# Splitting the first attention's projections into three fp32r products each

## The reference

```
xn = rmsnorm(h, attn_norm[0])                   # 256 x 1024
proj = xn @ fox_w_in                            # 1024 x (3*1024 + 16)
q, k, v = 16 heads of 64 each; f_logit = last 16 columns + b_f
cum = cumsum(log_sigmoid(f_logit), axis=tokens)
s = q @ k.T / 8 + (cum[t] - cum[s]), causal softmax, o = p @ v
h = h + o @ fox_w_o                             # 1024 x 1024
h = h + (silu(hn @ w_gate) * (hn @ w_up)) @ w_down      # hn = rmsnorm(h, ffn_norm[0]), width 2816
```

## Time and profile before

| | |
|---|---|
| Median of 3 runs | 1963.29 us (1955.23 to 1964.63) |
| Profiled execution | 1963.11 us, span 1961.3 us |
| TensorE busy | 1734.0 us, 88% of the span |
| VectorE busy | 1019.6 us, 52% |
| ScalarE busy | 510.2 us, 26% |
| GpSimd busy | 279.1 us, 14% |
| Mean granted clock of TensorE | 0.949 of full |

### The profile page before, as it was taken

The page is one execution under the profiler, slowest core; times in us unless marked ns, Lnnn a source line. Parts: engine busy times, 40 slices in busy tenths (PEclk is TensorE's granted clock), DMA queues, the critical chain, the costliest instruction groups (busy, mean ns, idle before and its releaser), DMA issues.

```text
span 1961.3 us, 22190 instructions
## 1 busy us (share of the span) xinstructions
PE 1734.0 (88%) x7497; PEld 1181.4 (60%) x7497; DVE 1019.6 (52%) x2438; ACT 510.2 (26%) x1012; POOL 279.1 (14%) x264
## 2 busy tenths in 40 slices
PE   7998999889989999799999899968878889788876
PEld 4784999856648999587565468543434434344332
DVE  1234555533435554445734311377776667776765
ACT  1342444212324443143211001122222212222222
POOL 0000000000000000000000000045434343333540
PEclk8999999999998999899999999989989999898998
DMA  5253566501336565133322325099999999999996
GB/s 173 77 169 103 167 192 183 167 16 44 96 103 181 180 184 182 31 126 124 105 110 80 115 78 189 25 371 420 420 421 421 422 421 421 421 421 421 422 421 255
DMA packets 209713, 435.30 MB, mean 222 GB/s; under 512 B 11649, under 2 KB 145153, under 8 KB 175745
## 3 DMA queue, kind: packets, MB, share of 16 engines
q0 software_dynamic: 36864, 268.45, 33.0%
q1 hardware_dynamic: 171760, 166.06, 26.5%
q10 hardware_dynamic: 1040, 0.13, 0.0%
HBM read 433.53 MB, written 1.05 MB: 222 GB/s over the span
## 4 chain that ended last, share of the span: by engine, by line
PE 72%; DMA 16%; DVE 7%; issue 3%; ACT 1%; POOL 0%; DVEq 0%; SPq 0%; POOLq 0%; ACTq 0%
PE ps L484 40%; DMA OT<-in_peer_uv,IX 15%; PE ps L1220 11%; PE ps L645 6%; PE ps L925 3%; PE ps L938 2%; PE ps L515 2%; PE ps L549 1%; PE ps L490 1%; PE ps L1135 1%; DVE SLOT L2277 1%; PE ps L1017 1%; DVE AR L1992 1%; PE ps L556 1%; DMA XT<-in_w_pq_by_head 0%
## 5 line engine op out<-in xcount | busy, mean ns | idle before, releaser
L1595 POOL DMA_INDIRECT SLOT<-in_peer_uv,IX x128 | 136.1, 1064 | 1520.2 <-DVE IX L2271 1276.0
L1220 PE MATMUL ps<-SLOT,AR 128*128 128x512 f32 x512 | 263.8, 671 | 96.6 <-ACT AR L1549 96.6
L484 PE MATMUL ps<-ARH 128*128 128x256 f32 x2112 | 261.0, 286 | 7.6 <-DVE ARH L1710 7.6
L484 PEld LDWEIGHTS ps<-ARH 128*128 128x128 f32 x2112 | 260.2, 195 | 9.5 <-issue 7.9
L1220 PEld LDWEIGHTS ps<-SLOT,AR 128*128 128x128 f32 x512 | 108.1, 216 | 245.9 <-issue 129.6
L2277 DVE SCALAR_TENSOR_TENSOR SLOT<-SLOT,V 128x1024 f32<-128x1024 f32 x128 | 153.3, 1224 | 77.4 <-DMA SLOT<-in_peer_uv,IX 75.4
L484 PE MATMUL ps<-XT,SLOT 128*128 128x256 f32 x832 | 183.2, 380 | 2.2 <-DVE XT L1659 1.3
L1710 DVE TENSOR_TENSOR ARH<-SLOT,ARH 128x2048 fp32r<-128x2048 f32 (+1 forms) x88 | 154.1, 1756 | 49.3 <-ACT ARH L1298 32.5
L484 PEld LDWEIGHTS ps<-XT,SLOT 128*128 128x128 f32 x832 | 157.4, 190 | 25.2 <-issue 3.7
L1220 PE MATMUL ps<-AR 128*128 128x512 f32 x320 | 144.6, 601 | 12.1 <-ACT AR L1549 12.1
L484 PE MATMUL ps<-SLOT,XT 128*128 128x512 f32 (+3 forms) x384 | 148.5, 547 | 4.0 <-DVE XT L1659 2.6
(11 more groups left out here) (338 smaller groups left out, 2119.4 us busy)
## 6 DMA issues: line engine op xcount, KB each, us to landing
SLOT<-in_w_gate SPq DMA_DIRECT2D x44, 512.0 KB, 4.0
SLOT<-in_w_up SPq DMA_DIRECT2D x44, 512.0 KB, 5.3
SLOT<-in_w_down SPq DMA_DIRECT2D x44, 512.0 KB, 5.2
SLOT<-in_w_in SPq DMA_DIRECT2D x9, 2048.0 KB, 8.6
SLOT<-in_fox_w_in SPq DMA_DIRECT2D x16, 512.0 KB, 3.9
XT<-in_w_pq_by_head SPq DMA_DIRECT2D x8, 1024.0 KB
SLOT<-in_mla_w_uq SPq DMA_DIRECT2D x8, 576.0 KB
SLOT<-in_fox_w_in SPq DMA_DIRECT2D x2, 2048.0 KB, 13.2
```

The costliest lines, as they stand in the source:

```text
L484: m = pe.matmul(outp, l, r, start=(n_ == 0), stop=(n_ == len(pairs) - 1))
L1220: m = pe.matmul(ps[:, 2 * t + c, :], DIAG[:, j, :], v_row(j)[:, c * 512:(c + 1) * 512], start=False, stop=False)
L1595: pool.indirect_dma_start(PAIR[j], None, pairs, bass.IndirectOffsetOnAxis(IX[:, t, j:j + 1], 0)).then_inc(gathered[j], 16)
```

## The change

Every projection of the first attention (logits, values, queries, keys, output) becomes a sum of three fp32r products. The parts are made as follows.

- The normalized input: ScalarE multiplies PSUM by the gain straight into the high part, and VectorE computes PSUM times gain minus the high part into the low part. XT and XT2, seen as fp32r, hold the two. The first and second feed-forward inputs are made in the same way, without the float32 copy between.
- Weights: GpSimd copies each into a high part in the arena (`HIGH`). VectorE overwrites the slot with the low part for the value weights and all pairs. For the output weights GpSimd makes both parts, one quarter per pair.
- The attention output of a pair: ScalarE copies the turned pair to the high part, VectorE subtracts for the low part.

A pair's two weight blocks now share one slot, so that pairs alternate between SLOT0 and SLOT1; the first two are loaded ahead of `cumt_ready`, and the output weights ahead of pair 2. The logits are computed with the 16 weight columns standing in the array, as 16 x 256, and transposed back between the two halves of the first value columns. The loops over pairs are written out on TensorE, ScalarE and VectorE; SP's too. The core of the diff:

```diff
+            def pair(i):
+                w = slot(i % 2, 2, KC, P)
+                fill(i % 2, (w[:, 0], rows(fw, i * P, i * P + P)), (w[:, 1], rows(fw, D + i * P, D + i * P + P)))
+            pair(0)
+            pair(1)
             sp.wait_ge(sem("cumt_ready"), 1)
             ...
             sp.dma_start(KT[0:16, 1, :], CUMT).then_inc(sem("negcum_here"), 16)
-            qk(rows(fw, 0, P), rows(fw, D, D + P))
-            with T.loop("fox", PAIRS - 1) as i:
-                qk(dyn(fw, i * P + P), dyn(fw, i * P + (D + P)))
             two_tiles(a["fox_w_o"][0])
+            for i in range(2, PAIRS):
+                pair(i)
...
+            def row_thirds(s, banks, X, n, between=None):
+                parted(s, n)
+                for t in range(NT):
+                    take(banks[t])
+                    group(ps[:, banks[t], :], tile_thirds(X, t, s, range(KC))).then_inc(full["v"][banks[t]], 1)
+                    T.add(free["v"][banks[t]])
+                    if t == 0 and between:
+                        between()
+                release(s)
...
-            row_tile(3, (2, 3), XT)
+            row_thirds(3, (2, 3), XHL, 4)
             evacuated(2, 3)
...
+            for i in range(PAIRS - 1):
+                fox_scores()
+                fox_proj(i + 1)
+                fox_attend(i)
             fox_scores()
+            parted(2, 4)
+            evacuated(7)
...
+            fox_attend(PAIRS - 1)
+            fox_turn()
+            evacuated(7)
...
+            release(2)
+            row_thirds(3, (2, 3), OTHL, 4)
...
+            def high_norm(dst, name):            # ScalarE
+                for g in range(4):
+                    act.wait_ge(full["a"][g], T.next(full["a"][g]))
+                    for k in (2 * g, 2 * g + 1):
+                        m = act.activation(dst[:, k, :], ps[:, g, k % 2 * S:k % 2 * S + S], ACT.Copy, scale=gcol(name, k, 1))
+                    m.then_inc(sem("norm_high"), 1)
...
+            def quarter(s, g, low=False):        # GpSimd
+                if g == 0:
+                    pool.wait_ge(here[s], T.next(here[s], 16))
+                ks = slice(2 * g, 2 * g + 2)
+                raw = view(SLOT[s][:], KC, 512)[:, ks, :]
+                if not low:
+                    pool.tensor_copy(HIGH[s][:, ks, :], raw).then_inc(weight_high, 1)
+                    return
+                pool.tensor_copy(HIGH[s][:, ks, :], raw).then_inc(sem("pool_high"), 1)
+                pool.wait_ge(sem("pool_high"), T.next(sem("pool_high")))
+                pool.tensor_tensor(view(SLOTR[s][:], KC, 512)[:, ks, :], raw, HIGH[s][:, ks, :].bitcast(F32), ALU.subtract).then_inc(split[s], 1)
+            for s in (2, 3):
+                for g in range(4):
+                    quarter(s, g)
+            for n_ in range(PAIRS):
+                p = n_ % 2
+                pool.wait_ge(here[p], T.next(here[p], 32))
+                pool.tensor_copy(HIGH[p], view(SLOT[p][:, 0:2 * KC * P], 2, KC, P)).then_inc(weight_high, 1)
+                quarter(2 + n_ // 4, n_ % 4, low=True)
...
+            def low_norm(dst, high, name):       # VectorE
+                for g in range(4):
+                    dve.wait_ge(sem("norm_high"), T.next(sem("norm_high")))
+                    for k in (2 * g, 2 * g + 1):
+                        m = STT(dst[:, k, :], ps[:, g, k % 2 * S:k % 2 * S + S], gcol(name, k, 1), high[:, k, :].bitcast(F32), ALU.mult, ALU.subtract)
+                    m.then_inc(free["v"][g], 1)
...
+            low_norm(XHL[1], XHL[0], "attn0").then_inc(sem("xh_ready"), 1)
+            low_quarters(2)
             dve.wait_ge(full["v"][4], T.next(full["v"][4]))
+            dve.tensor_copy(CUMT[:], ps[0:16, 4, 0:S]).then_inc(free["v"][4], 1)
+            low_quarters(3)
...
             signal("cumt_ready")
+            low_pair(0)
+            low_pair(1)
             values(lambda c, t: 2 * c + t)
...
+            for i in range(PAIRS):
                 fox_scores(i)
+                attend_tail(i, between=(lambda: low_pair(i + 2)) if i + 2 < PAIRS else None)
+                if i:
+                    turned_low(i - 1)
+            turned_low(PAIRS - 1)
```

More of the change, by code:

```diff
@@ L667, in _, with logits_back @@
             release(0)
-            norm_t()
+            norm_t("a")
             pe.wait_ge(sem("wf_here"), T.next(sem("wf_here"), 32))
             take(4)
-            for t in range(NT):
-                m = group(ps[:, 4, 16 * t:16 * t + 16], ((cols(XT, t, k), WF[:, k, :]) for k in range(KC)))
-            m.then_inc(full["v"][4], 1)
+            pe.wait_ge(sem("xh_ready"), T.next(sem("xh_ready")))
+            group(ps[0:16, 4, 0:S], sum((thirds(lambda h: (WFH, WFL)[h][:, k, :], lambda h: XHL[h][:, k, :]) for k in range(KC)), [])).then_inc(full["v"][4], 1)
             T.add(free["v"][4])
-            row_tile(2, (0, 1), XT)
+            def logits_back():
+                evacuated(4)
+                take(5)
+                for t in range(NT):
+                    m = pe.transpose(ps[:, 5, 16 * t:16 * t + 16], CUMT[:, t * P:(t + 1) * P], IDENT[0:16, 0:16])
+                m.then_inc(full["v"][5], 1)
+                T.add(free["v"][5])
+            row_thirds(2, (0, 1), XHL, 4, between=logits_back)
             pe.wait_ge(sem("logf_ready"), T.next(sem("logf_ready")))
@@ L690, in _, with fox_proj, fox_turn, fox_attend @@
             T.add(free["v"][5])
-            row_tile(3, (2, 3), XT)
+            row_thirds(3, (2, 3), XHL, 4)
             evacuated(2, 3)
-            def fox_proj():
+            def fox_proj(i):
+                p = i % 2
+                parted(p, loads=2)
+                w = (HIGH[p], low_of(p, 2, KC, P))
                 for s_, b in ((0, 0), (1, 6)):
                     take(b)
-                    pe.wait_ge(here[s_], T.next(here[s_], 16))
-                    group(ps[:, b, 0:S], ((slot(s_, KC, P)[:, k, :], XT[:, k, :]) for k in range(KC))).then_inc(full["a"][b], 1)
+                    group(ps[:, b, 0:S], sum((thirds(lambda h: w[h][:, s_, k, :], lambda h: XHL[h][:, k, :]) for k in range(KC)), [])).then_inc(full["a"][b], 1)
                     T.add(free["a"][b])
-                    release(s_)
+                release(p)
+            def fox_turn():
+                evacuated(5)
+                take(7)
+                for t in range(NT):
+                    m = tr(ps[:, 7, t * P:(t + 1) * P], ON[:, t, :])
+                m.then_inc(full["a"][7], 1)
+                T.add(free["v"][7])
+            def fox_attend(i):
+                flip(0)
+                flip(1)
+                mix_values(i, 0)
+                if i:
+                    fox_turn()
+                mix_values(i, 1)
             def fox_scores():
@@ L1313, in ffn @@
                 root()
-                for g in range(4):
-                    act.wait_ge(sem("xt_ready"), T.next(sem("xt_ready")))
-                    act.copy(XH[:, 0, 2 * g:2 * g + 2, :], XT[:, 2 * g:2 * g + 2, :]).then_inc(sem("high_ready"), 1)
+                high_norm(XH[:, 0], f"ffn{l}")
                 for b in range(2):
```

152 lines of the change are left out of this document (88 added, 64 removed).

## The result

The changed kernel takes 1941.66 us (median of 7 runs, 1939.72 to 1947.66). The kernel before took 1955.91 us in the 7 runs beside them, and 1960 to 1963 in the larger sets later. The ratio is 0.9919 [0.9899, 0.9939] (worked out from all the runs, not from the two medians), so the change is faster by 0.6 to 1.0%, 12 to 20 us. The forecast of 1954 us (1944 to 1969) lies 12 us above the measured time, which is 2 us outside its range. The profiled execution took 1941.62 us, 21.5 less than the one of before; its span is 1939.5 us at a mean clock of 0.955 (0.949 before).

The account below looks back on a forecast made before the run. The prediction took TensorE, busy 88% of the span, as the bound wherever it finishes last. Its terms, +6.5 + 0.5 - 7.8 - 1.9 + 0.4 - 3.1 - 3.4 = -8.8 us, took 1963.1 to 1954.3, stated as 1954 (1944 to 1969).

Parts of the forecast that it names:

- Front, +6.5: Before the first pair's projection: TensorE idles some 10 us for the value copies, then runs at half clock; +6.5 us.
- All three signs that were to overturn the forecast: Idle time at the front under 4 or over 16 us, GpSimd's 2048 copy over 4 us, pitch above 11.2.
- Log-sigmoid is hidden: At the front, during the value columns: the log-sigmoid work costs TensorE no wait; no term in the sum.
- Late second pair, +0.5: Start of the pair loop: scores of pair 1 come 1 us late, against 2.5 us of slack; +0.5 us.
- pair loop, -7.8: Seven pair projections: three fp32r products replace two fp32 instructions, -1.12 us each, pitch about 10.55; -7.8 us.
- Output projection, -4.6: End of the attention: cheaper products -1.9 and -3.1 us, an extra VectorE difference in the last turn +0.4 us.
- Feed-forward input, -3.4: From turning to first gate matmul in both heads: operands made from PSUM come 1.7 us earlier, twice; -3.4 us.
- If the shorter gap also spared the half clock behind it, 96 x 0.014 = 1.3 more each: Gate matmuls behind each feed-forward input: a possible further 1.3 us each, not counted in the sum.
- Later stages see no edit and only shift: Everything behind the edited stages: unchanged apart from moving in time; no term in the sum.
- Rival A: Front: the new wait doesn't show, so -5.5 instead of +6.5 there and 1942 us in all; chance 0.12.
- Rival B: Front and pair loop: GpSimd becomes the bound, with VectorE and GpSimd excluding one another; 1970 to 1981 us; chance 0.15.
- Rival C: TensorE's clock gives the gain back: 6 us lost, feed-forward heads gain nothing (2 us); 1962 us; chance 0.18.

Follow-up runs that it names:

- e8: The changed kernel with 18 unread float32 matmuls filling TensorE's wait ahead of the first pair's projection: 1941.83 us.
- e3: The changed kernel with the value copies moved ahead of VectorE's low part of pair 1: 1930.77 us, ratio 0.9848.
- e1: The kernel before with only the two feed-forward inputs made the new way: 1948.07 us, ratio 0.9937.
- e4: The kernel of e1 with two unused VectorE additions ahead of the signal, giving both heads the old gap length: 1965.13 us, ratio 1.0002.
- e10: The changed kernel with two redundant GpSimd copies of 2048 elements in each pair from the third on: 1954.63 us in its one run.
- e2: The changed kernel with the feed-forward inputs made as before, so the attention change alone: 1956.26 us, ratio 0.9968.
- e13: The kernel of e1 with the old gap length back in the first feed-forward input only: 1953.16 us, ratio 0.9965.
- e12: The kernel of e1 with four VectorE additions at its start, meant to delay everything by 2.8 us: 1951.07 us, ratio 0.9956.
- e11: The kernel before with four VectorE additions at its start, meant to delay everything by 2.8 us: 1959.29 us, ratio 1.0011.
- e5: The kernel before with six unread float32 matmuls in TensorE's gap in each feed-forward head: 1958.86 us, ratio 0.9969.
- e9: The kernel of e3 with two more front reorderings, plus five filler matmuls ahead of and five behind the turning in both feed-forward inputs: 1933.58 us, ratio 0.9862.

## Why the prediction was wrong, step by step

- **Front, +6.5: right in mechanism and nearly in size.** All three signs that were to overturn the forecast stayed away (8.6 us idle, 1.88 us for GpSimd's copy of 2048, a pitch of 10.1), so its error is not in the attention. Scores of pair 0 went from 64.78 to 69.99, +5.2. GpSimd was faster than assumed (1.04 us for a copy of 1024, 1.88 for 2048, against 1.3 and 2.6); the subtraction took 2.36 instead of 2.0, a little over the 2.25 that the prediction estimated from the Trainium skill (GPSIMD Engine Reference, performance versus the Vector engine). "Log-sigmoid is hidden" was wrong: TensorE waits 2.11 us for the log gates (37.55 in the fence of the front), but the values had started at 23.55 and not at 25, so the load of the output weights still went out in time. The half clock cost more than forecast: from the projection's start to the first scores it took 9.53 us (60.46 to 69.99), and 7.03 in e8 at full clock (60.22 to 67.25), so 2.5 instead of 1.8. e3 undid the wait and gained 11 us; the forecast's price between waiting and not waiting was 12.
- **Late second pair, +0.5, and pair loop, -7.8.** Scores of pair 0 to scores of pair 7 took 81.20 us before (64.78 to 145.98) and 71.39 after: -9.8 where -7.3 was forecast. The pitch is (141.38 - 100.99) / 4 = 10.10 instead of 10.55. Three products take (87.46 - 82.52) / 14 = 0.353 us in the second projection's timeline, 0.118 each, not the 0.124 read from a group with mixed neighbours; that is 0.3 a pair, and 0.15 is left over.
- **Output projection, -4.6.** Last scores to last residual: 35.54 us before, 31.61 after (172.99), -3.9. With the front and the loop this makes -8.5 at the last residual, where the terms had -5.4.
- **Feed-forward input, -3.4: the step that failed.** The gap shrank from 3.79 to 2.57 or 2.60 us, 1.2 and not 1.7, so by the gaps it is -2.4. But the term is mostly a matter of clock, which the sum put at nothing: "If the shorter gap also spared the half clock behind it, 96 x 0.014 = 1.3 more each" stood as a remark, outside the sum, and it looked only at the first head. The second, of which no row stands in the prediction, had a turning of 6.74 us (2.9 over the 3.84 at full clock) and gates of 14.30 (2.5 over). The two heads alone measure -12.4 us (8 to 17, e1), and lose all of it when the gap is given back (e4). In place of -3.4 stand 2.4 us of shorter gaps and 17 us less at half clock in an average run, which is up to 8.5 us.
- **"Later stages see no edit and only shift": wrong.** Between the first gates and the second turning the lead of the profiled execution grew by 3.6 us and behind the second head's gates by 1.7, where no instruction changed. Its half-clock stretches lie elsewhere than in the profile of before; how much of that belongs to the change and how much to the single execution isn't shown.
- **Rival A** fell (the wait is there). Its number, 1942, is the measured time, by coincidence: the wait that it left out is there, and the gain came elsewhere. **Rival B** fell for this kernel: 7.2 us a pair. Its exclusion is real (last section), and e10 shows the loop following GpSimd once that needs 11.1 us a pair. **Rival C** was half right. The half clock at the front came (54 to 66 us), and the attention alone runs 11 us longer at half clock than before (e2). But it said that the heads gain nothing, and there the clock gave more than the attention lost; over the whole kernel TensorE has 5 to 8 us less of it. No rival had the clock as a gain; that was the missing case, and the dips in the earlier trace rows were in view.

**What stays open.** Which idle time the chip answers with half clock. The gap's length moves the mean over runs (e1, e4, e13, e12 against e11), and filling the old gap works in part (e5). Filling elsewhere gave nothing that the runs could tell (e8, e9). Single executions differ even where code and moment are the same (18.77 and 18.72 us), and no run shows what decides there.

**A better version.** Values ahead of pair 1's low part (e3) takes 1930.77 us, 0.9848 of before and 11 us less than the changed kernel, with one line moved.

## What to carry to other kernels

Count TensorE's half-clock time in the profile before you forecast, at every repetition of a stage, and give the clock a term with both signs: two waits of TensorE that became 2.4 us shorter in all were worth 12 here (8 to 17). Take the clock from many executions and not from one profile: single runs of one kernel had 160 to 200 us of half clock. Filler work did not replace a shorter wait: at the old gap it won 6 us where the shorter gap won 12, and in two other places nothing that the runs could tell. When one engine prepares operands for two consumers, look at what stands behind the wait in its queue: moving four copies ahead of one waiting instruction was worth 11 us, more than the attention's whole change by itself (6.3).

## What the runs showed of the hardware

GpSimd's cast from float32 to fp32r takes 1.04 us for 1024 elements a partition and 1.88 for 2048, 0.9 ns an element, faster than VectorE's two-input subtraction (2.28 us for 2048). GpSimd and VectorE hold each other up where VectorE subtracts with both inputs in SBUF. In the fence of the front the same GpSimd subtraction takes 2.36 us alone and 4.27 beside VectorE's of 2048 elements. That one takes 3.09 us instead of 2.28 (alone, at 39.83 us), and the cast in front of GpSimd's subtraction (54.69, 1.03 us) lies over its start. At the value weights casts and subtractions do the same (timeline of the changed kernel, four at a time, first slot and second): in the first slot the casts are nearly over when VectorE begins, in the second they overlap.

```profile
15.03 3.99 POOL L1680 CAST ARH<-SLOT 128x1024 fp32r<-128x1024 f32 x4 [12.94 <-DMA SLOT<-in_fox_w_in]
18.20 5.30 DVE L1823 TENSOR_TENSOR SLOT_R<-SLOT,ARH 128x1024 fp32r<-128x1024 f32 x4
25.05 5.99 POOL L1680 CAST ARH<-SLOT 128x1024 fp32r<-128x1024 f32 x4 [6.03 <-DMA SLOT<-in_fox_w_in]
26.13 8.83 DVE L1823 TENSOR_TENSOR SLOT_R<-SLOT,ARH 128x1024 fp32r<-128x1024 f32 x4 [2.30 <-POOL ARH L1680]
```

The Trainium skill (SBUF — State Buffer, who interferes with whom) says that a VectorE instruction with two SBUF inputs contends with a GpSimd instruction that reads SBUF. The trace agrees, and its times add up as if one waited for the other: VectorE's 2.28 behind the end of the cast (55.72) would end at 58.0, and it ends at 57.86; GpSimd's 2.36 behind that would end at 60.2, and it ends at 60.07.
